# A fused two-block forward pass: norms whose roots are made on one column, spread and turned by TensorE

## The reference

```python
def rmsnorm(x, g):
    xf = xf * lax.rsqrt(jnp.mean(xf * xf, axis=-1, keepdims=True) + NORM_EPS)
    return xf * g

mem_n = rmsnorm(mem, mem_norm)
h = x
h = h + hybrid_mixer(rmsnorm(h, norm_mix), ...)        # has grouped norms too
h = h + memory_cross_attention(rmsnorm(h, norm_xa), mem_n, ...)
h = h + swiglu(rmsnorm(h, norm_ffn), ...)
h = rmsnorm(h, norm_final)
# second block: norm_mix_2 (its eps 1e-6), three mixers, swiglu, last norm

def grouped_rmsnorm(x, g, n_groups):    # in the mixer: 4 groups of 512, and 16 of 128
    xf = x.reshape(..., n_groups, -1)
    xf = xf * lax.rsqrt(jnp.mean(xf * xf, axis=-1, keepdims=True) + NORM_EPS)
```

## The kernel before

| norm | product | mean, root | inverse |
|---|---|---|---|
| 0 | step 8 | 9 | 10 |
| 1 | 224 | 225 | 226, turned 228 |
| 2 | 248 | 249 | 250 |
| 3 | 280 | 281 | 282 |
| 4 | 540 | 541 | 542, second 542 and 543 |
| 5 | 640 | 641 | 642 |
| grouped | 152, 168, 200, 213 | +2 | +3 |

## Time and profile before

### The profile page before, as it was taken

The page is one execution under the profiler, slowest core; times in us unless marked ns, Lnnn a source line. Parts: engine busy times, 40 slices in busy tenths (PEclk is TensorE's granted clock), DMA queues, the critical chain, the costliest instruction groups (busy, mean ns, idle before and its releaser), DMA issues.

```text
span 2657.6 us, 38786 instructions
## 1 busy us (share of the span) xinstructions
PE 2630.5 (99%) x15098; PEld 2278.8 (86%) x15098; DVE 1961.8 (74%) x2903; ACT 1500.3 (56%) x2315; POOL 404.6 (15%) x390
## 2 busy tenths in 40 slices
PE   9999999999999999999999999999999999999998
PEld 7888888888799888888888888888888888888887
DVE  7777777978877765666666698687877777777775
ACT  6555658686556444444444465545565555555555
POOL 2111003225201010000000053011101010101012
PEclk9999999999999999999999999999999999999999
DMA  6555565566556555666666666546566656666654
GB/s 232 185 187 184 177 198 187 181 206 192 169 174 194 175 158 169 189 191 190 190 190 190 190 189 202 168 127 190 183 195 189 190 189 191 190 190 191 190 183 134
DMA packets 136703, 490.78 MB, mean 185 GB/s; under 512 B 15431, under 2 KB 16520, under 8 KB 136520
## 3 DMA queue, kind: packets, MB, share of 16 engines
q1 hardware_dynamic: 136088, 487.78, 59.0%
q10 hardware_dynamic: 432, 0.52, 0.1%
HBM read 486.12 MB, written 2.13 MB: 184 GB/s over the span
## 4 chain that ended last, share of the span: by engine, by line
PE 94%; DVE 4%; ACT 1%; issue 1%; DMA 1%; SPq 0%; DVEq 0%; ACTq 0%
PE ps L831 59%; PE ps L828 29%; DVE wl L1361 1%; DMA raw<-in_w_sc 1%; PE ps L1003 0%; PE ps L845 0%; ACT wh L1067 0%; PE ps L1036 0%; PE ps L1025 0%; DVE XM L1367 0%; PE ps L955 0%; DVE X L1367 0%; PE ps L816 0%; PE ps L815 0%; PE ps L814 0%
## 5 line engine op out<-in xcount | busy, mean ns | idle before, releaser
L831 PE MATMUL ps<-X,wh 128*128 128x512 f32 x4848 | 1628.0, 397 | 7.0 <-DVE wl L1361 3.7
L1361 DVE TENSOR_TENSOR wl<-raw,wh 128x1024 fp32r<-128x1024 f32 (+1 forms) x905 | 1174.2, 1300 | 456.9 <-ACT wh L1067 456.3
L1067 ACT ACTIVATE wh<-raw 128x1024 fp32r<-128x1024 f32 (+1 forms) x905 | 954.6, 1057 | 663.2 <-PE ps L828 624.5
L828 PE MATMUL ps<-X,wl 128*128 128x256 f32 x4848 | 1220.3, 279 | 0.0
L831 PEld LDWEIGHTS ps<-X,wh 128*128 128x128 f32 x4848 | 889.5, 188 | 202.6 <-issue 9.0
L828 PEld LDWEIGHTS ps<-X,wl 128*128 128x128 f32 x4848 | 881.6, 188 | 29.4
L831 PE MATMUL ps<-XG,wh 128*128 128x512 f32 x2176 | 733.4, 397 | 7.4 <-DVE hT L1361 7.4
L828 PE MATMUL ps<-XG,wl 128*128 128x256 f32 x2176 | 548.4, 279 | 0.0
L831 PEld LDWEIGHTS ps<-XG,wh 128*128 128x128 f32 x2176 | 397.3, 189 | 90.7 <-DVE hT L1361 9.6
L828 PEld LDWEIGHTS ps<-XG,wl 128*128 128x128 f32 x2176 | 398.6, 189 | 16.3
L1840 POOL TENSOR_TENSOR hT<-hT,T 128x256 f32<-128x256 f32 x224 | 193.1, 884 | 1411.6 <-DVE hT L1361 1411.4
(11 more groups left out here) (198 smaller groups left out, 1257.1 us busy)
## 6 DMA issues: line engine op xcount, KB each, us to landing
raw<-in_w_gate SPq DMA_DIRECT2D x176, 512.0 KB, 3.8
raw<-in_w_down SPq DMA_DIRECT2D x176, 512.0 KB, 3.7
raw<-in_w_sc SPq DMA_DIRECT2D x95, 512.0 KB, 4.2
raw<-in_w_up SPq DMA_DIRECT2D x88, 512.0 KB, 3.7
raw<-in_w_val SPq DMA_DIRECT2D x88, 512.0 KB, 3.7
raw<-in_w_zx SPq DMA_DIRECT2D x80, 512.0 KB, 4.1
raw<-in_w_in SPq DMA_DIRECT2D x68, 512.0 KB, 3.7
raw<-in_w_osc SPq DMA_DIRECT2D x32, 512.0 KB, 3.7
```

The costliest lines, as they stand in the source:

```text
L828: t = e.matmul(bank(c, i)[:, 0:256], wl[:, b0:b0 + 128], X[:, kx * 512:kx * 512 + 256], start=False, stop=sp and kk == c.kn - 1)
L831: e.matmul(bank(c, i)[:, :], wh[:, b0:b0 + 128], X[:, kx * 512:kx * 512 + 512], start=st and kk == 0, stop=False)
L1067: return e.activation(out, in_, ACT.Copy, scale=scale)
L1361: return e.tensor_tensor(out, a, b, op)
```

## The change

1. x and mem come also by position (`xtok`, `mtok`, two DMAs of 1 MB each). `tsq` squares 2048 channels in one ScalarE operation per half of the positions, with the sum in a column. `nsq`, `nmm` and GpSimd's sums go for norms 0 and 1. mem's norm moves from steps 215 to 229 to steps 18 to 23; its gains (`mgain`) are put anew, in the order MORD.
2. For norms 2 to 5, the second root of norm 4 and the grouped ones, the product has the squares as weights and one column of ones as data: a sum for each position, by partition, one column per half.
3. Mean, root and inverse are made on 128x2.
4. `nbc`: ScalarE multiplies a tile of ones by each column (two of 128x128). `ntr`: TensorE turns both into a bank. `nrs`: ScalarE copies the bank into RS. `snb`, `snt`, `snc` are the same for the grouped norms, `nbc2`, `ntr2`, `nrs2` for the second root. `nfinb`, `nbc` and `ntr` stand in the same step.
5. `evs` of the columns that come too early for the new factor moves behind it, with what follows it. v takes its factor from the column, so `memT` and `memc` go.

```diff
+    def root(step, ni):
+        put(step, "nfin", ni)
+        for piece in ("nfinb", "nbc", "ntr"):
+            put(step + 1, piece, ni)
+        put(step + 2, "nrs", ni)
+
+    for ni, step in ((0, 8), (1, 18)):
+        for st in range(2):
+            if ni:
+                put(step - 6 + st, "tload", st)
+            put(step + st, "tsq", (ni, st))
+        root(step + 2 + ni, ni)
...
-                put(b + 11, "sn1b", g)
-                s = max(b + 12, U_OSC[g // 2] + 1)
+                for piece in ("sn1b", "snb", "snt"):
+                    put(b + 11, piece, g)
+                put(b + 12, "snc", g)
+                s = max(b + 13, U_OSC[g // 2] + 1)
...
-                    put(e + 4, "nfin", ni)
-                    put(e + 5, "nfinb", ni)
+                    root(e + 4, ni)
...
-                    put(e + 6, "nfin2b", 0)
+                    for piece in ("nfin2b", "nbc2", "ntr2"):
+                        put(e + 6, piece, 0)
+                    put(e + 7, "nrs2", 0)
...
-        at[step].sort(key=lambda p: p[0] not in ("ev", "res", "resn", "vcopy"))
+        at[step].sort(key=lambda p: p[0] not in ("ev", "res", "resn", "vcopy", "nrs", "nrs2"))
...
+                    if i in (4, 5):
+                        e.dma_start(tok(i - 4), T_["xtok"][:, 2048 * (i - 4):2048 * (i - 3)]).then_inc(d_tok[i - 4], 16)
...
-                    e.matmul(b[:, 0:256], ones[:, :], a0, start=True, stop=False)
-                    w.wait_ge(fold, i + 1)
-                    c7 = RN[i][7] if i > 1 else None
-                    e.matmul(b[:, 0:256], ones[:, :], sq_of(i, 7, c7)[:, 0:256], start=False, stop=True).then_inc(nmm, 1)
+                    for st in range(2):
+                        e.matmul(b[:, st:st + 1], a0[:, 128 * st:128 * st + 128], ones[:, 0:1], start=True, stop=False)
+                        w.wait_ge(fold, i - 1)
+                        t = e.matmul(b[:, st:st + 1], a7[:, 128 * st:128 * st + 128], ones[:, 0:1], start=False, stop=True)
+                    t.then_inc(nmm, 1)
...
+                if piece == "ntr":
+                    w.wait_ge(d_ident, 16)
+                    w.wait_ge(nbc, i + 1)
+                    for st in range(2):
+                        t = turn(nbank(i)[:, 256 + 128 * st:384 + 128 * st], spread(i)[:, 128 * st:128 * st + 128])
+                    t.then_inc(ntr, 1)
...
+                if piece == "tsq":
+                    ni, st = i
+                    w.wait_ge(d_tok[st], 16 * ni + 16)
+                    e.activation(tok(st), tok(st), ACT.Square, accum_out=col_of(ni, 6 + st, 1)).then_inc(tsq, 1)
...
+                if piece == "nbc":
+                    w.wait_ge(nv, 5 * i + 5)
+                    if i > 1:
+                        w.wait_ge(nmm, i - 1)
+                    for st in range(2):
+                        t = copy(spread(i)[:, 128 * st:128 * st + 128], ones[:, :], col_of(i, 4 + st, 1))
+                    t.then_inc(nbc, 1)
+                if piece == "nrs":
+                    w.wait_ge(ntr, i + 1)
+                    w.wait_ge(evS, [0, 0, EVN[of("z")[7].n], EVN[of("k")[1].n], EVN[of("q")[1].n], EVN[of("gu")[2].n]][i])
+                    copy(rsb(i), nbank(i)[:, 256:512]).then_inc(nrs, 1)
...
+                if piece == "snb":
+                    w.wait_ge(snv, 5 * i + 5)
+                    for st in range(2):
+                        t = copy(sacc(i)[:, 128 * st:128 * st + 128], ones[:, :], cols_sn(i, 4)[:, st:st + 1])
+                    t.then_inc(snb, 1)
...
-                    y, u = rsb(i), tile(10 if i == 1 else 8)
+                    v, u, y = col_of(i, 0), col_of(i, 2), col_of(i, 4)
```

More of the change, by code:

```diff
@@ L515, in program @@
         "sq2", "acc2", "fold2", "nmm2", "fA", "fv", "hA", "hP", "og", "opre"))
-    s_ones, s_pad, s_gg, mtP, memc_s, vc = (sem(n) for n in ("ones", "pad", "gg", "mtP", "memc", "vc"))
+    s_ones, s_pad, s_gg, vc = (sem(n) for n in ("ones", "pad", "gg", "vc"))
+    d_tok, tsq, nbc, ntr, nrs = [sem(f"d_tok{i}") for i in range(2)], sem("tsq"), sem("nbc"), sem("ntr"), sem("nrs")
+    snb, snt, snc = (sem(n) for n in ("snb", "snt", "snc"))
     cG, bG, bsq, gn, brA, br = (sem(n) for n in ("cG", "bG", "bsq", "gn", "brA", "br"))
@@ L682, in conv_of, with col_of, col2, cols_sn @@
                 "gate": (2, "fc_w", 88, n - 44, "fc_b"), "up": (2, "fc_w", 88, n, "fc_b")}[c.kind]
+    def col_of(ni, a, n=2):
+        return vT[:, 64 + 8 * ni + a:64 + 8 * ni + a + n]
+    def col2(a):
+        return vT[:, 112 + a:114 + a]
+    def cols_sn(g, a):
+        return vT[:, 120 + 8 * g + a:122 + 8 * g + a]
+    def nbank(ni):
+        return banks[4 if ni in (2, 4, 5) else 6]
+    def spread(ni):
+        return tile(8 if ni == 0 else 10 if ni == 1 else 9)
     def norm_gain(ph, k):
@@ L820, in unit @@
                     X, kx, s, n = xtile(c, g * c.kn + kk)
[L821 to L824, removed]
+                    if u == 0:
+                        w.wait_ge(lo, kk + 1)
                     w.wait_ge(s, n)
@@ L859, in tensor @@
                 if piece == "nmm":
[L860 to L864, removed]
+                    b, a0, a7 = nbank(i), tile(8), sq_of(i, 7, RN[i][7])
+                    w.wait_ge(acc, 7 * i - 7)
                     if i == 2:
@@ L907, in tensor @@
                     t.then_inc(nmm, 1)
-                if piece == "memT":
-                    w.wait_ge(nv, 10)
-                    w.wait_ge(s4, 16)
-                    turn(banks[5][:, 0:128], rsb(1)[:, 0:128])
-                    turn(banks[5][:, 128:256], rsb(1)[:, 128:256]).then_inc(mtP, 1)
                 if piece == "bmm":
@@ L961, in tensor @@
                     if i:
-                        w.wait_ge(snv, 5 * (i - 1) + 1)
-                    e.matmul(banks[6][:, 0:256], ones[:, :], sacc(i), start=True, stop=True).then_inc(snm, 1)
+                        w.wait_ge(snc, i)
+                    for st in range(2):
+                        t = e.matmul(banks[6][:, st:st + 1], sacc(i)[:, 128 * st:128 * st + 128], ones[:, 0:1], start=True, stop=True)
+                    t.then_inc(snm, 1)
+                if piece == "snt":
+                    w.wait_ge(snb, i + 1)
+                    for st in range(2):
+                        t = turn(banks[6][:, 256 + 128 * st:384 + 128 * st], sacc(i)[:, 128 * st:128 * st + 128])
+                    t.then_inc(snt, 1)
                 if piece == "att0":
@@ L1075, in scalar @@
                 if piece == "split0":
-                    w.wait_ge(d_w0[i], 16)
-                    copy(wh[:, 256 * i:256 * i + 256], raw[:, 256 * i:256 * i + 256]).then_inc(hi if i == 3 else hi0, 1)
+                    w.wait_ge(d_part[i], 16)
+                    copy(wh[:, 256 * i:256 * i + 256], raw[:, 256 * i:256 * i + 256]).then_inc(hi, 1)
                 if piece == "split":
@@ L1268, in scalar @@
                     w.wait_ge(snv, 5 * i + 1)
-                    e.activation(sacc(i), vT, ACT.Sqrt).then_inc(snA, 1)
+                    e.activation(cols_sn(i, 2), cols_sn(i, 0), ACT.Sqrt).then_inc(snA, 1)
+                if piece == "snb":
+                    w.wait_ge(snv, 5 * i + 5)
+                    for st in range(2):
+                        t = copy(sacc(i)[:, 128 * st:128 * st + 128], ones[:, :], cols_sn(i, 4)[:, st:st + 1])
+                    t.then_inc(snb, 1)
+                if piece == "snc":
+                    w.wait_ge(snt, i + 1)
+                    if i > 1:
+                        w.wait_ge(yv, 4 * (i - 1))
+                    else:
+                        w.wait_ge(s_pad, 1)
+                    copy(srs(i), banks[6][:, 256:512]).then_inc(snc, 1)
                 if piece == "sn2h":
@@ L1985 @@
     arr["memT"] = fm(I["mem"][0])
+    for n, v in (("xtok", I["x"][0]), ("mtok", I["mem"][0])):
+        arr[n] = np.ascontiguousarray(v.reshape(2, 128, 2048).transpose(1, 0, 2)).reshape(128, 4096)
     rc = np.ones((4, 16), f)
```

260 lines of the change are left out of this document (118 added, 142 removed).

## The result

The changed kernel takes 2671.95 us (median; 2671.74 to 2675.15) against 2658.72 before: ratio 1.0053, 95% interval 1.0035 to 1.007, so 13 us slower. Forecast were 2674 and a range of 2660 to 2687. The profiled execution spans 2669.9 us where that of before spans 2657.6, so 12.3 us are to be found between the two traces. Two executions, one of before at 5275 us and one of run 5 at 7478, are left out of all ratios here.

What follows compares the result with a forecast made beforehand. TensorE, busy 2630.5 of 2657.6 us, was taken as the bound. Added waits and slow clock of 34.6 us less 19.7 saved made 14.9 us slower, about 2674 us, range 2660 to 2687.

Steps and rivals of the forecast that it cites:

- the stretch from 637.91: Units 213 to 229, 14.1 us too long: long DVE operations, GpSimd's sums and ScalarE's squares go, saving 13.4 us.
- the stretch from 1596.91: Units 540 to 549, 8.4 us too long: 6.3 saved; norm 4's two roots add waits of 2.3 and 2.0 us.
- norms 2, 3, 5: TensorE waits 1.9 us for each root's turns; with the reordered and slower units, 2.3 us each.
- grouped norms: Steps 155, 171, 203 and 216: waits for turns behind table loads and earlier roots cost 2.5, 1.8, 2.3 and 5.0 us.
- norm 0: Start-up: extra DMA and wide squares make TensorE wait 6 us before unit 12; 3.5 us slower with order and clock.
- norm 1: Steps 18 to 22, ScalarE's fullest place: 5.8 us idle, 0.5 for turns and order, 2.0 for the clock, 8.3 in all.
- rival C: The clock falls at the eight short waits too, 11 us more: 2685 us; chance 0.12.
- step 216: Fourth grouped norm: 3.4 us with turns and reordering, plus 1.5 for the half clock behind the wait, 5.0 taken.
- Rival E: Spread copies are ready when TensorE arrives, eleven places cost 0.5 us each, the start gains 3: 2642 us; chance 0.08.
- B: The two early norms are cheap: norm 0 waits only 2 us, norm 1 costs 2.3: 2662 us; chance 0.18.
- D: Units 213 to 229: the rest of DVE's work keeps half the waits, 10 us not saved: 2684 us; chance 0.07.

Runs made afterwards that it cites:

- run 5: Kernel before, with six of mem's eight squares on ScalarE and their GpSimd additions done on 2 columns instead of 512: 2654.61 us, ratio 0.9981.
- run 1: Changed kernel, with the root at all eleven places at the front of its step, ahead of eviction and split, turns unmoved: 2649.76 us, ratio 0.9962.
- run 2: Changed kernel, with the turns of all eleven places behind the next unit and the copy back behind that step's split: 2648.91 us, ratio 0.9960.
- run 3: Changed kernel, with two more 128-column ScalarE copies ahead of the two spread copies at all eleven places: 2685.06 us, ratio 1.0092.
- run 4: Kernel before, with each of its eleven 128 x 256 reciprocals replaced by a short multiply-and-add writing a constant: 2651.15 us, ratio 0.9967.
- run 6: Kernel before, with both cuts at once, short operations for reciprocals and six of mem's squares and additions on 2 columns: 2646.10 us, ratio 0.9948.
- run 8: Changed kernel, with TensorE multiplying ones by ones during the waits before the turns of norms 0, 1 and the fourth grouped norm: 2668.73 us, ratio 1.0033.
- run 9: Changed kernel, norms' turns behind the next unit, grouped roots and norms 0 and 1's roots in front, mem's norm at steps 43 to 48: 2646.05 us.
- run 10: As run 9, but with norm 0's root behind its step's eviction and split again: 2644.47 us, ratio 0.9944.
- run 7: Changed kernel, with mem's norm alone moved from steps 18 to 23 to steps 43 to 48: 2671.46 us, ratio 1.0044.

## Why the prediction was right, step by step

Each row compares the prediction's term with what the change added between the two profiled executions, read from the starts of the same units (norm 0 between units 8 and 19, norm 1 between 19 and 27). It is one execution of each kernel.

| step of the prediction | forecast | measured |
|---|---|---|
| the stretch from 637.91 (measured: units 219 to 229) | -13.4 | -13.4 |
| the stretch from 1596.91, with both roots of norm 4 in it | -6.3 + 4.3 | -2.4 |
| norms 2, 3, 5 | 2.3 each | 2.2, 2.1, 2.1 |
| grouped norms | 2.5, 1.8, 2.3, 5.0 | 2.8, 1.7, 2.4, 5.5 |
| norm 0 | +3.5 | +2.0 |
| norm 1 | +8.3 | +7.2 |
| sum | +14.9 | +12.3 (rows: 12.2) |

**The waits.** The chain at norm 2 was worked out from rows of the kernel before, split end to turn, as 1.9 us behind the unit's end; it took 769.07 - 767.15 = 1.92, turns included. Runs 1 and 2 show that the order is the cause and run 3 that the copies are on the path. At the grouped norms the same addition held to 0.5. All eleven waits stand where the prediction put them: nine of 1.3 to 3.5 us, and 4.8 and 5.2 at the early norms, where it had two near 6.

**The savings.** Their size was right. My reason was DVE's ten long operations, GpSimd's sums and ScalarE's squares as one lump; runs 4 to 6 part it, and the reciprocals, the most visible piece, are less than a quarter of it in the first stretch. So the size was right without the parts having been priced.

**The early norms** were over-estimated by 1.5 and 1.1. For norm 0 each step of the chain came 0.3 to 1.1 us earlier than written: I had the wide squares at about 2.0 and they are 1.90, the start was not held by the DMA as long, and unit 12 began at 47.93, not 48.75. These two rows are the whole of what the forecast had too much; the others cancel. For norm 1 ScalarE's timeline of the changed kernel shows the links in the order in which I had walked them, each within 0.8 us of its time:

```profile
69.94 1.28 ACT L1252 ACT_TABLE_LOAD   x1
...
71.88 1.28 ACT L1254 ACT_TABLE_LOAD   x1
...
74.67 1.90 ACT L1148 ACTIVATE A<-A 128x2048 f32<-128x2048 f32 x1
...
79.72 1.28 ACT L1173 ACT_TABLE_LOAD   x1
82.97 0.20 ACT L1173 ACTIVATE T<-T 128x2 f32<-128x2 f32 x1 [1.97 <-DVE T L1430]
...
86.07 0.69 ACT L1110 ACTIVATE T<-ones,T 128x128 f32<-128x128 f32 x2 [1.95 <-DVE T L1433]
```

From the start of unit 18 at 67.17 the spread ends at 19.6 us against my 19.9; the wait is 5.2 against 5.8, and the clock took 1.3 against 2.0. One link the walk does not name: the table load was through at 81.00, and the root waited 1.97 us more for the mean, which on DVE stood behind a column's additions and scalings and a split, and itself took longer than the 0.16 of norm 0:

```profile
82.23 0.70 DVE L1430 TENSOR_SCALAR T<-T 128x2 f32<-128x2 f32 x1
```

My 16.2 for "copy, table load and root" had 1.2 us in it that those three do not need, so the end came out right.

**The clock.** Past the start-up the changed kernel dips behind the three waits named, and again only at the last norm (0.51 of the clock from 2660 us on), as the kernel before does (0.50 from 2650 us on). That the eight short waits kept the clock was partly luck, and rival C was nearer than my 0.12 says: run 3 crossed over with 0.6 us more a wait, and in run 8 the clock fell behind 2.30 and 1.61 us at two of these very places. My sentence that by the rule of the Trainium skill nothing would be added at step 216 was a misreading: the idle time that I forecast there (652.9 less 649.7, 3.2 us) is one of the long gaps that the rule warns of. **Rival E** needed the root 1.5 us earlier; run 1 made it so, and its 2649.8 lies above E's 2642 by the early norms, which I had let E have for nothing. **Rivals B and D** fall: the early norms waited 4.8 and 5.2 us where B had some 2, and of the waits at units 219 to 229, of which D kept half, none is left.

## What to carry to other kernels

Where a result goes through several engines and back into the one that bounds the kernel, its place in that engine's order matters more than the length of the operations: write down when the chain's input is there, add the links, and put the last one behind work that lasts as long. A shorter operation whose start is tied to the same event as before gained nothing at norm 2, and the links that came with it cost 2.2 us. Where DVE was what TensorE waited for, the shorter operation was worth something by itself: the old kernel with a short operation in place of each reciprocal, and no new links, was 8.7 us faster (run 4), the change as made 13 slower. Before a chain is put ahead of an eviction or a split, look at who waits for those. The root at the front of its step was worth 1.7 us at norm 2; at norm 0 it shortened the wait by 2.3 us while the turns stood behind the same unit (run 1), and once they stood a unit later it made the next unit wait 1.5 us longer for its bank (run 9 against run 10).

## What the runs showed of the hardware

The length of a wait does not by itself say whether TensorE's granted clock falls to its lower level (0.5 of the 2.4 GHz, 1.2 GHz) behind it. The same piece in the same order, before unit 156: 2.31 us idle in the changed kernel and the unit behind at 1.00 (3.98 us), 2.30 us idle in run 7 and the unit at 0.69 (5.52 us). Before unit 217: 3.47 us and 0.61 in the changed kernel, 3.48 us and 1.00 in run 7. Two rows of run 7:

```profile
476.49:482.01 5.52, 5.52 (x29) 4.41 (x27) 2.54 (x3) 2.65 (x6) 1.42 (x2) 0.69 0.39 123
...
670.56:673.44 2.88, 2.88 (x18) 2.53 (x18) 2.02 (x3) 0.97 (x2) 0.00 (x0) 1.00 0.14 55
```

Between the start-up and the last norm the shortest wait behind which it fell was 1.61 us (run 8, the unit at 624.27; at the same place it held behind 1.62 in the changed kernel), the longest behind which it held 3.48. So my added 1.5 us at step 216 was the right price in one execution and too much by all of it in another. The Trainium skill ("TensorE: Matmul & The Clock Gate", section "Why this matters for your kernels") asks that long gaps between bursts be avoided; that filling them helps, run 8 shows, but the length of a gap alone, by which the rule goes, sorts these cases wrongly both ways. What decides it stays open: no run here was made to find out. Each such fall cost 1.2 to 2.4 us; the executions of the changed kernel lie 3.4 us apart, so one or two falls more or less could make that spread, which no run shows.
